# Moving the optional blocks of a mixture-of-experts loop into its middle

## The reference, cut to what matters

```python
def _moe(h, router_w, router_b, w_gate_up, b_gate_up, w_down, b_down):
    hf = h.reshape(bsz * seq_len, d)                     # 256 tokens that count, d = 1024
    logits = (hf @ router_w + router_b).astype(jnp.float32)
    top_val, top_idx = lax.top_k(logits, TOP_K)          # 4 of 32
    ...
    for e in range(N_EXPERTS):
        gu = hf @ w_gate_up[e] + b_gate_up[e]            # 1024 x 2048, f32: 8 MB
        g, lin = gu[:, :D_EXPERT], gu[:, D_EXPERT:]
        g = jnp.minimum(g, SWIGLU_LIMIT)
        lin = jnp.clip(lin, -SWIGLU_LIMIT, SWIGLU_LIMIT)
        act = g * jax.nn.sigmoid(SWIGLU_ALPHA * g) * (lin + 1.0)
        out = out + combine[:, e:e + 1] * (act @ w_down[e] + b_down[e])   # 1024 x 1024: 4 MB
    return out.reshape(bsz, seq_len, d)
```

## Time and profile before

| | us |
|---|---|
| median of three runs | 1180.0 |
| the profiled execution | 1180.36 |
| its span, from first to last instruction | 1178.6 |
| PE busy | 986.5 (84%) |
| VectorE busy | 321.2 (27%) |
| ScalarE busy | 131.2 (11%) |
| mean DMA rate over the span | 369 GB/s |
| DMA rate in the slice from 265 to 295 us | 70 GB/s |

### The profile page before, as it was taken

The page is one execution under the profiler, slowest core; times in us unless marked ns, Lnnn a source line. Parts: engine busy times, 40 slices in busy tenths (PEclk is TensorE's granted clock), DMA queues, the critical chain, the costliest instruction groups (busy, mean ns, idle before and its releaser), DMA issues.

```text
span 1178.6 us, 23769 instructions
## 1 busy us (share of the span) xinstructions
PE 986.5 (84%) x10044; PEld 457.6 (39%) x10045; DVE 321.2 (27%) x951; ACT 131.2 (11%) x292; POOL 14.9 (1%) x26
## 2 busy tenths in 40 slices
PE   8999999898986666669999996699766898876695
PEld 6887886332432222223334332234222333322232
DVE  5999942421211111112222121112111121111112
ACT  2211230510000000000000000000000000000002
POOL 1111000000000000000000000000000000000000
PEclk9999999898998788789999999899978999998898
DMA  9763686791999999999899999999999999999994
GB/s 260 227 168 109 239 320 276 277 418 70 428 426 427 426 426 427 426 425 386 344 409 400 427 427 426 426 426 426 426 426 425 426 426 426 426 426 426 426 426 199
DMA packets 69355, 434.87 MB, mean 369 GB/s; under 512 B 15232, under 2 KB 31552, under 8 KB 36560
## 3 DMA queue, kind: packets, MB, share of 16 engines
q1 hardware_dynamic: 69184, 434.41, 90.0%
q10 hardware_dynamic: 144, 0.09, 0.0%
HBM read 431.69 MB, written 1.05 MB: 367 GB/s over the span
## 4 chain that ended last, share of the span: by engine, by line
PE 43%; DMA 41%; DVE 9%; SPq 4%; issue 3%; ACT 0%; ACTq 0%; DVEq 0%
DMA ring<-in_w_down 21%; DMA ring<-in_w_gate_up 17%; PE ps L1472 17%; PE ps L1485 8%; DMA early<-in_w_gate_up 4%; PE ps L1356 2%; PE ps L1407 2%; PE ps L1218 2%; SPq L369 2%; PE ps L1438 2%; PE ps L1461 2%; PE ps L1429 2%; SPq L366 2%; PE ps L1372 1%; PE ps L1454 1%
## 5 line engine op out<-in xcount | busy, mean ns | idle before, releaser
L1472 PE MATMUL ps<-ring,base 128*32 128x512 f32 x2208 | 293.2, 674 | 125.6 <-DMA ring<-in_w_gate_up 96.6
L1472 PEld LDWEIGHTS ps<-ring,base 128*32 128x32 f32 x2208 | 69.7, 117 | 320.1 <-issue 177.2
L1485 PE MATMUL ps<-ring,base 128*32 128x256 f32 x2944 | 177.2, 381 | 12.9 <-DMA ring<-in_w_down 12.4
L1485 PEld LDWEIGHTS ps<-ring,base 128*32 128x32 f32 x2944 | 88.8, 110 | 102.8 <-ACT base L699 38.6
L1133 DVE TENSOR_SCALAR base<-ps 128x256 f32<-128x256 f32 x46 | 19.5, 424 | 378.0 <-PE ps L1472 378.0
L1218 PE MATMUL ps<-ring 128*128 128x256 f32 (+1 forms) x448 | 103.5, 390 | 0.0
L1218 PEld LDWEIGHTS ps<-ring 128*128 128x128 f32 x448 | 85.1, 192 | 15.4 <-issue 1.4
L697 ACT ACTIVATE base<-base 128x256 f32<-128x256 f32 x46 | 19.1, 416 | 637.2 <-DVE base L1133 637.2
L1089 DVE TENSOR_TENSOR base<-ps,base 128x256 f32<-128x256 f32 x47 | 19.9, 424 | 203.5 <-PE ps L1447 203.5
L1472 PE MATMUL ps<-late,base 128*32 128x512 f32 x368 | 51.1, 678 | 16.6 <-DMA late<-in_w_gate_up 16.6
L1472 PE MATMUL ps<-early,base 128*32 128x512 f32 x368 | 50.0, 666 | 15.4 <-DMA early<-in_w_gate_up 15.4
(11 more groups left out here) (329 smaller groups left out, 688.9 us busy)
## 6 DMA issues: line engine op xcount, KB each, us to landing
ring<-in_w_gate_up SPq DMA_DIRECT2D x96, 2048.0 KB, 38.9
ring<-in_w_down SPq DMA_DIRECT2D x63, 2048.0 KB, 40.7
late<-in_w_gate_up SPq DMA_DIRECT2D x16, 2048.0 KB, 40.5
early<-in_w_gate_up SPq DMA_DIRECT2D x16, 2048.0 KB, 39.8
ring<-in_w_in SPq DMA_DIRECT2D x14, 1024.0 KB, 7.8
ring<-in_w_out SPq DMA_DIRECT2D x4, 1024.0 KB, 14.5
ring<-in_w_s_lin SPq DMA_DIRECT2D x2, 1024.0 KB, 6.6
ring<-in_w_s_gate SPq DMA_DIRECT2D x2, 1024.0 KB, 5.1
```

The source lines that it names most:

```text
L1472: ins = nc.tensor.matmul(ps[BS * q:BS * q + BS, 0, :].rearrange("p (a c) -> p a c", a=2), xT[:, k % 2, k // 2, :], row[:, :, QW * q:QW * q ...
L1485: ins = nc.tensor.matmul(ps[BS * q:BS * q + BS, 1, 0:QW], actT[:, n % 2, n // 2, :], row[:, out_cols(q)], start=(n == 0), stop=(n == KT - ...
```

## The change: what it does

A constant `HEAD` (16) and a register `rest` (`total` - 16) are new. On each of the three engines the loop over blocks 0 to 31 becomes a loop over blocks 0 to 15; the tested groups now run blocks 16 to `total` - 17, with the same tests; and a new, third loop runs the last 16 blocks, `rest` to `total` - 1. The order of the blocks, what each computes, and SP's code are the same. For 46 blocks the tested groups run 14 blocks in both kernels: 32 to 45 before, 16 to 29 now.

```diff
+HEAD = EXP // 2
+        blk_rest = base[96:97, 248:249].bitcast(I32)
@@ VectorE, ahead of the loops
+            nc.vector.tensor_scalar(blk_rest, ps[0:1, 3, 64 + EXP - 1:64 + EXP], -float(EXP - HEAD), None, ALU.add)
@@ PE (ScalarE and VectorE alike, with their loops from 0)
+            rest = pe.value_load(blk_rest[0:1, 0:1], min_val=HEAD, max_val=NBLK - (EXP - HEAD))
-            with pe.Fori(1, EXP) as i:
+            with pe.Fori(1, HEAD) as i:
                 one_block(i)
-            with pe.Fori(0, (NBLK - EXP) // TURNS) as turn:
+            with pe.Fori(0, (NBLK - EXP + 1) // TURNS) as turn:
                 with pe.If(EXP + turn * TURNS < total):
                     with pe.Fori(0, TURNS) as t:
                         with pe.If(EXP + turn * TURNS + t < total):
-                            one_block(EXP + turn * TURNS + t)
+                            one_block(HEAD + turn * TURNS + t)
+            with pe.Fori(0, EXP - HEAD) as j:
+                one_block(rest + j)
             pe.wait_ge(y_ready, total + 1)
             pe.wait_ge(selT_ready, total + 1)
             scatter().then_inc(scattered, 1)
```

More of the change, by code:

```diff
@@ L693, in _ @@
             total = act.value_load(blk_total[0:1, 0:1], min_val=EXP, max_val=NBLK)
+            rest = act.value_load(blk_rest[0:1, 0:1], min_val=HEAD, max_val=NBLK - (EXP - HEAD))
             def one_block(i):
@@ L702, in one_block @@
                 selection(i + 1)
-            with act.Fori(0, EXP) as i:
+            with act.Fori(0, HEAD) as i:
                 one_block(i)
-            with act.Fori(0, (NBLK - EXP) // TURNS) as turn:
+            with act.Fori(0, (NBLK - EXP + 1) // TURNS) as turn:
                 with act.If(EXP + turn * TURNS < total):
@@ L709, in _ @@
                         with act.If(EXP + turn * TURNS + t < total):
-                            one_block(EXP + turn * TURNS + t)
+                            one_block(HEAD + turn * TURNS + t)
+            with act.Fori(0, EXP - HEAD) as j:
+                one_block(rest + j)
             link(nc.scalar.activation(ss[:, 15:16], ss[:, 14:15], ACT.Sqrt))
@@ L1109, in _ @@
             total = dve.value_load(blk_total[0:1, 0:1], min_val=EXP, max_val=NBLK)
+            rest = dve.value_load(blk_rest[0:1, 0:1], min_val=HEAD, max_val=NBLK - (EXP - HEAD))
             def one_block(i):
@@ L1142, in one_block @@
                 nc.vector.tensor_copy(ysb, ps[:, 1, 0:QW]).then_inc(y_ready, 1)
-            with dve.Fori(0, EXP) as i:
+            with dve.Fori(0, HEAD) as i:
                 one_block(i)
-            with dve.Fori(0, (NBLK - EXP) // TURNS) as turn:
+            with dve.Fori(0, (NBLK - EXP + 1) // TURNS) as turn:
                 with dve.If(EXP + turn * TURNS < total):
@@ L1149, in _ @@
                         with dve.If(EXP + turn * TURNS + t < total):
-                            one_block(EXP + turn * TURNS + t)
+                            one_block(HEAD + turn * TURNS + t)
+            with dve.Fori(0, EXP - HEAD) as j:
+                one_block(rest + j)
             def sums(c, half):
```

## The result

The changed kernel took 1182.09 us (median of 20 runs, 1180.46 to 1186.38) against 1179.1 us (20 runs, 1176.58 to 1181.06): slower by a ratio of 1.003, 95% interval 1.002 to 1.0039. The direction was the forecast one, and the size less than half of it: +3.0 us where +7.3 was forecast. (The forecast of 1187.3 us stood on the 1180.0 of three runs; the 20 runs of before give 1179.1.) The profiled execution has a span of 1180.5 us, 1.9 more than the one of before.

A forecast was written before the change was run, and what follows sets the result against it. PE's pace up to block 19's start was taken to bound all later weights: 0.5 + 0.8 + 5.8 + 2.65 = +9.75 us there, -2.4 at the end, net +7.3, giving 1187.3 us; range 1181.5 to 1192 (8 in 10).

The forecast's parts named there:

- What bounds the kernel: PE sets the pace in blocks 14 to 19; whatever delays block 19's start delays every later weight by as much.
- Tests: Each tested block costs 0.27 us more idle; blocks 17, 18 and 19 pay +0.8 us where PE sets the pace.
- Entering the groups: Ahead of block 16, heads of two loops and two tests: 0.5 us, bounds 0 and 2.0 us.
- The end: Blocks 44 and 45 save 0.5 us without tests, the scatter after the last down product 1.9 us: -2.4 us.
- Code that has not run yet: PE jumps past a never-run even body and stalls ahead of block 17: 5.8 us, bounds 0 and 12.8.
- The clock after the stall: Block 17 runs once at TensorE's lower clock after the stall: +2.65 us, bounds 0 and 2.65.
- The extra register: Register read on three engines and a small VectorE instruction ahead of the loops: nothing; uncovered 0.2 to 0.5 us.
- half a stall: Rival: code piece under way when PE jumps ahead of block 17; 2.9 us, slow clock, +4.4, 1184.4 us; chance 0.12.
- two pieces in a row: Rival: block 17's jump and the next stretch each fetch a piece, 6.4 us more, +13.7, 1193.7 us; chance 0.08.

The follow-up runs named there:

- head24: Changed kernel with HEAD = 24 instead of 16, so tested groups run blocks 24 to 37; 1177.78 us against 1178.35 for the kernel before, ratio 0.999.
- padded kernels: 64 or 128 idle instructions added at the start of PE's program: kernel before 1181.91 and 1195.37 us, changed kernel 1187.98 and 1201.72 us.
- second profile: The changed kernel run once more, unaltered, for its spread; 1184.20 us.
- before_again2: The kernel before run again unaltered, the second of two further profiles for its spread; 1178.68 us.
- others_only: Against the kernel before, only VectorE and ScalarE run the blocks in three loops, PE keeps its two; 1178.28 us, ratio 1.0007.
- before_pad3: The kernel before with three idle instructions at the start of PE's program; 1176.89 us against 1177.91, ratio 0.9993.

## Why the prediction was wrong in size, point by point

*What bounds the kernel* held: block 19's start carried the whole rest with it, since from there to block 44's it is 509.9 to 510.3 us in every profile of every kernel here, and head24 shows the cover for such stalls.

*Tests*: forecast 0.27 us each, measured 0.33 to 0.39 (1.04 against 0.65, 0.71 against 0.38). *Entering the groups*: forecast 0.5, measured 46.86 - 46.27 = 0.59. *The end*: forecast -2.4, measured -1.95 at the scatter and -0.45 ahead of blocks 44 and 45.

*Code that has not run yet* is the first step that failed, in size: I put the stall at 5.8 us "between the two", ordering its price by how loaded the DMAs are, and took what I had measured for the fetch of one piece ("6.4 each"). Block 16 became 4.07 us longer, of which about 0.3 is a test, so the stall cost 3.8, less than either of the two prices. The packets show what was there in its place: two pieces, 3.2 us apart, the first of them starting just as PE falls idle and not 1.5 us later, as by block 2 of the kernel before. The padded kernels show that how many packets there are and when the first comes goes by where the jump and its target lie in the code: the same jump, under much the same load, costs up to 2.1 us more. *The clock after the stall* failed with it: forecast 2.65, the full price, measured 17.86 - 15.76 - 0.35 = 1.75 us here, where the clock was back sooner, and 2.4 in the second profile. Together with the small terms, block 19 came 7.08 us late against block 13 and not 9.75.

*The extra register* is the second step that failed: "I put them at nothing". It does two things. Reading it stands on PE's path: the idle time ahead of block 1 grew from 0.93 to 1.57 us, and block 0 took 17.45 us where before_again2, at the same clock of 1.00, took 16.82. And PE's three more instructions shift the first loop too: the stall ahead of block 2, which sits in both kernels in a stretch where PE sets the pace, was 5.3 to 5.7 us in three profiles of before and in others_only, where PE does not read the register, and is 4.1 to 4.5 in all seven profiles where PE reads it and has no idle instructions added. before_pad3 does this without any register: 4.33 us idle and 1.0 us less in the median, though its interval just reaches no change. Blocks 1 and 2 of the changed kernel's two profiles are 2.3 and 0.8 us shorter than before's 38.83, the rest of it clock.

The sum of the profiled pair: +0.65 to block 0's start, -1.19 in block 0 (+0.6 for the register, and the clock, by which before's own profiles vary by 1.97), -2.56 in blocks 1 and 2, +0.33 from block 3 to 13, +7.08 to block 19, -0.25 to block 44, -0.23 in block 44 and -1.95 at the end: +1.9, the difference of the spans. For the medians: 7.3 forecast, less 2.0 for the stall, 0.9 for the clock and about 1.0 for block 2, plus 0.3 for tests and entry and 0.6 for the register read, leaves 4.3, against 3.0 measured. A further 0.2 us stands outside the span: kernels in which VectorE and ScalarE have the third loop take 2.0 us more than their span on average, the others 1.7 to 1.8. So 1.5 us stay open, less than the clock alone moves block 0.

The rival "half a stall" (2.9 us and a full slow clock, +4.4) came nearest in time, but its mechanism, a piece already well under way when PE jumps, is not what the packets show: the first starts as PE falls idle. Of "two pieces in a row" the two packets are there, at half the price that it gave each. That the time came near a rival's is no merit of that rival. Why the pieces are asked for when they are I can't show; what the runs show is the dependence on position.

## What to carry to other kernels

Before moving a loop or adding a copy of a body, look at what the first pass of existing code costs ("issue" idle with packets in the code queue), and ask at which place of the run the new copy is first entered: under a transfer it was free at 10 us, ahead of a step that releases transfers 4 us of it reached the end. Splitting off the last blocks to get their tests out of the end let the scatter start 2 us sooner behind the last product in each profile of a kernel that does so on PE. With the split put into the DMAs' stage the kernel was faster than before, though by 0.6 us in the median only. Even three instructions ahead of a loop can move such a stall by 1 us, so changes of this size have to be compared against a padded original.

## What the runs showed of the hardware that I had not expected

- The stall at a first jump past a body of 377 matmuls and weight loads was between 2.9 and 6.8 us by position in the code, with no position of those tried near 1 us. Ahead of block 17 it held two or three packets of code, 3.2 to 3.4 us apart; with the DMAs at 426 GB/s the packets stood 5.9 and 6.2 us apart.
- An idle instruction that only raises a semaphore is not free, at about 0.16 us: 64 of them delayed PE's block 0 by 5.6 us and 128 by 15.3 us, although PE had 5 us to wait there.
- A copy just entered by its even body can stall again when that body follows: 7.1 and 7.2 us ahead of block 13 with HEAD = 12, in two profiles of two, and 7.2 us ahead of block 27 in one of the two.
- After a stall the first 32 gate and up instructions took 5.0 to 6.8 us instead of 3.64; the mean granted clock of blocks 16 to 18, with a stall ahead of block 17, was 0.91 to 0.97 by execution and kernel.
